# A dense feed-forward block by one level of Strassen's scheme, and a rare branch of the experts with semaphores of its own

## The reference, cut to what matters

```python
def swiglu(t, w_gu, w_down):                 # w_gu: 1024 x 5632, w_down: 2816 x 1024
    a, g = jnp.split(t @ w_gu, 2, axis=-1)
    return (jax.nn.silu(a) * g) @ w_down

def first_block(...):
    ...
    for l in range(DEPTH):                   # DEPTH = 2
        ... mixer, cross attention ...
        if l % 2 == 0:
            f = swiglu(h, ffn_w_gu[l // 2], ffn_w_down[l // 2])
        else:
            f = moe_swiglu(h, moe_router[l // 2], moe_w_gu[l // 2], moe_w_down[l // 2])
        h = layer_norm(ALPHA * h + f, ln_g[l, 2], ln_b[l, 2])

def moe_swiglu(h, w_router, w_gu, w_down):   # 8 experts, 2 for each token
    ...
    for e in range(N_EXPERTS):
        out = out + gate[:, e:e + 1] * swiglu(t, w_gu[e], w_down[e])
```

## Time and profile before

| | us |
|---|---|
| median of three runs | 2226.9 (2225.84 to 2227.3) |
| profiled execution, its own time | 2227.21 |
| profiled execution, span from first to last instruction | 2225.4 |
| TensorE busy in the span | 2157.3 |
| VectorE busy | 511.8 |
| ScalarE busy | 269.4 |
| GpSimd busy | 65.0 |

### The profile page before, as it was taken

One profiled execution on the slowest core, in us unless ns is written; L12 is line 12 of the kernel. 1 busy time (PEld: TensorE's weight loads), 2 busy tenths in 40 slices (PEclk: granted clock), 3 DMA queues, 4 the chain that ended last, 5 costly groups with the idle time before them and its releaser, 6 DMA issues.

```text
span 2225.4 us, 27297 instructions
## 1 busy us (share of the span) xinstructions
PE 2157.3 (97%) x12390; PEld 1211.5 (54%) x12390; DVE 511.8 (23%) x1050; ACT 269.4 (12%) x561; POOL 65.0 (3%) x70
## 2 busy tenths in 40 slices
PE   7999999999999999989999999999999799999998
PEld 3887665987458876753333333333333444854883
DVE  2413213001132232132001001101000489332021
ACT  1242001001013310010000000000000032420000
POOL 0000000000000000000000000000000035000000
PEclk9999999999999999999999999999999899999999
DMA  7524442433245244244999998799999542325240
GB/s 281 217 76 156 185 151 90 176 142 110 107 193 198 95 170 170 76 170 188 384 399 386 393 404 342 306 386 399 383 405 388 208 189 95 114 113 213 90 151 19
DMA packets 38422, 485.39 MB, mean 218 GB/s; under 512 B 4336, under 2 KB 4368, under 8 KB 6816
## 3 DMA queue, kind: packets, MB, share of 16 engines
q1 hardware_dynamic: 34976, 465.70, 52.6%
q0 software_dynamic: 3328, 17.90, 2.0%
HBM read 482.53 MB, written 1.05 MB: 217 GB/s over the span
## 4 chain that ended last, share of the span: by engine, by line
PE 95%; DVE 2%; DMA 1%; ACT 1%; issue 0%; DVEq 0%; SPq 0%; PEldq 0%
PE pair L335 50%; PE bank L335 46%; DMA weights<-in_w_in 0%; DMA weights<-in_even_in 0%; DVE att L1424 0%; DMA norm_par<-in_norms 0%; ACT hT L2255 0%; DVE hT L1424 0%; DVE att L2031 0%; ACT big L2239 0%; DVE stats L1476 0%; DVE h L1485 0%; DVE big L1424 0%; DVE h L1483 0%; DVE big L2013 0%
## 5 line engine op out<-in xcount | busy, mean ns | idle before, releaser
L335 PE MATMUL bank<-weights,att 128*32 128x512 f32 x4224 | 457.8, 593 | 0.0
L335 PE MATMUL pair<-weights,big 128*32 128x512 f32 (+1 forms) x1840 | 340.7, 592 | 1.6 <-DVE big L1911 1.6
L335 PE MATMUL pair<-hT,weights 128*128 128x256 f32 (+1 forms) x1600 | 310.3, 357 | 4.8 <-DVE hT L1424 3.9
L335 PEld LDWEIGHTS bank<-weights,att 128*32 128x32 f32 x4224 | 135.0, 110 | 306.4 <-issue 306.4
L335 PEld LDWEIGHTS pair<-hT,weights 128*128 128x128 f32 x1600 | 276.3, 192 | 38.9 <-DVE hT L1424 4.4
L335 PEld LDWEIGHTS pair<-weights,big 128*32 128x32 f32 (+1 forms) x1840 | 127.6, 129 | 204.5 <-issue 201.9
L335 PE MATMUL bank<-hT,weights 128*128 128x256 f32 x960 | 213.8, 382 | 0.0
L335 PEld LDWEIGHTS bank<-hT,weights 128*128 128x128 f32 x960 | 180.3, 190 | 31.5 <-issue 8.0
L335 PE MATMUL pair<-weights,hT 128*128 128x512 f32 (+1 forms) x448 | 190.6, 586 | 3.3 <-DMA weights<-in_w_in 1.9
L335 PEld LDWEIGHTS pair<-weights,hT 128*128 128x128 f32 x448 | 85.3, 191 | 104.5 <-issue 100.6
L1819 DVE TENSOR_TENSOR big<-head_gain,bank 128x256 f32<-128x256 f32 x66 | 27.8, 421 | 423.9 <-ACT head_gain L2369 423.9
(11 more groups left out here) (277 smaller groups left out, 1384.6 us busy)
## 6 DMA issues: line engine op xcount, KB each, us to landing
weights<-in_moe_up SPq DMA_DIRECT2D x88, 2048.0 KB, 10.7
weights<-in_moe_down SPq DMA_DIRECT2D x40, 2048.0 KB, 11.4
weights<-in_w_in SPq DMA_DIRECT2D x18, 2048.0 KB, 7.4
weights<-in_ffn_up SPq DMA_DIRECT2D x11, 2048.0 KB, 7.3
weights<-in_even_in SPq DMA_DIRECT2D x10, 2048.0 KB, 7.9
weights<-in_mem_wkv SPq DMA_DIRECT2D x8, 2048.0 KB, 7.3
weights<-in_odd_in SPq DMA_DIRECT2D x8, 2048.0 KB, 7.2
norm_par<-in_norms POOLq DMA_DIRECT2D x10, 1024.0 KB, 10.7
```

What stands on the lines that cost most here:

```text
L335: ins = pe.matmul(o, lhsT, rhs, **flags)
```

## The change

The dense block's chunks 2 to 10 are computed by one level of Strassen's scheme, in the form with seven products and fifteen sums. The tokens and the tile of weights are each cut into four blocks; the seven products have 128 moving columns, four tiles of the contraction and two halves of columns, so eight matmuls each. DVE makes four sums of the weights' blocks for each tile, one chunk ahead (`sums_of_tile`), and once four sums of the tokens' blocks (`sums_of_tokens`). The first tile's sums and the tokens' stand ahead of DVE's products for chunks 0 and 1. Some sums of products are left to PSUM, where products 6 and 7 add to the region of product 1 and product 3 to that of product 5; ACT copies the intermediate values out (`kept`), and DVE adds the rest.

In `dense_down` the pair of the second row tile is begun after the first row tile's matmuls of the first tile, and the wait for the last chunk moves to the last tile of weights.

The general path of the experts gets semaphores of its own (`all_filled`, `all_pair0_emptied`, `all0_used`, `all0_landed` and so on). The semaphores of the fast path then count only what it does, in TensorE, DVE and SP; its closing waits and counts on TensorE go, on DVE two of four waits and the counts. The slots' later counts are taken from `few_uses`, 17 for slots 0 and 1 and 34 for the others.

```diff
@@ TensorE: dense_ffn
                 for c in range(2, HID_CHUNKS):
-                    s = next_tile()
-                    o = begin(pairs, (name, "up", c))
-                    for i in range(2):
-                        for part in range(2):
-                            for k in range(KD):
-                                at = k * 512 + part * 256 + i * P
-                                ins = mm(o[:, i, part * T:(part + 1) * T], weights[:, s, at:at + P], hT[:, k, :],
-                                         start=(k == 0), stop=(k == KD - 1))
-                    end(ins)
-                    slot_owed[0] = f"slot{s}_used"
-                pe.wait_ge(*emptied((name, "up", HID_CHUNKS - 1)))
-                dense_down(name)
+                    seven_products(name, c)
+                dense_down(name)
+
+            def seven_products(name, c):
+
+                s = next_tile()
+                o = begin(pairs, (name, "up", c), late=True)
+                w, v = begin(banks, (name, "up", c, 2), late=True), begin(banks, (name, "up", c, 4), late=True)
+                regions = {"Y": o[:, 0, 0:256], "Z": o[:, 1, 0:256], "W": w[:, 0:256], "V": v[:, 0:256]}
+                tile = weights[:, s, :].rearrange("p (k n) -> p k n", n=512)
+                t1, t2, t4 = tile_sums[c % 2]
+
+                def one(label, region, tokens, block, start):
+                    if label not in (2, 4):
+                        jobs[name, "up", c, label] = jobs[name, "up", c]
+                    for i in range(2):
+                        for k in range(KD // 2):
+                            ins = mm(regions[region][:, i * P:(i + 1) * P], block[:, k, i * P:(i + 1) * P], tokens(k),
+                                     start=(start and (i, k) == (0, 0)),
+                                     stop=(k == KD // 2 - 1), skip_group_check=True)
+                    end_late(ins, (name, "up", c, label))
...
+                one(1, "Y", part(0, 0), tile[:, 0:4, 0:256], True)
+                one(2, "W", part(1, 0), tile[:, 4:8, 0:256], True)
+                pe.wait_ge(*L.next("sums_ready"))
+                if c == 2:
+                    pe.wait_ge(*L.next("token_sums_ready"))
+                one(5, "Z", total(0), t1, True)
+                one(4, "V", part(1, 1), t4, True)
+                pe.wait_ge(*L.next("first_kept"))
+                one(6, "Y", total(1), t2, False)
+                pe.wait_ge(*L.next("fifth_kept"))
+                one(3, "Z", total(3), tile[:, 4:8, 256:512], False)
+                pe.wait_ge(*L.next("sixth_kept"))
+                one(7, "Y", total(2), tile[:, 0:4, 256:512], False)
@@ TensorE: dense_down
-                outs = [begin(pairs, (name, "down", t), late=True) for t in range(NT)]
+                outs = []
...
                     for t in range(NT):
+                        if k0 == 0:
+                            outs.append(begin(pairs, (name, "down", t), late=True))
...
+                            if (t, i) == (0, 0) and k1 + nk == KF:
+                                pe.wait_ge(*emptied((name, "up", HID_CHUNKS - 1)))
@@ TensorE: moe, the end of the Else branch
                     few_sum(1)
-                    assert begun() == IN_FEW, begun()
-
-                    for i in range(2):
-                        for t in range(NT):
-                            pe.wait_ge(*emptied(("few_sum", 1, i, t)))
-                    pe.sem_inc(sems("banks_filled"), to_come("banks_filled", IN_FEW["banks_filled"]))
-                    for s in range(2):
-                        more = ALL_ROUNDS - few_count(FEW_ROWS - 2 + s, s)
-                        pe.sem_inc(sems(f"slot{s}_landed"), 16 * more)
-                        pe.sem_inc(sems(f"slot{s}_used"), more)
...
+                for s in range(NSLOT):
+                    after_few[s] = few_uses[s]
@@ VectorE: moe, the end of the Else branch
                     few_sum(1, row)
                     for i in range(2):
-                        for t in range(NT):
-                            ve.wait_ge(*emptied(("few_sum", 1, i, t)))
-                    for name, n in IN_FEW.items():
-                        if name != "banks_filled" and to_come(name, n):
-                            ve.sem_inc(sems(name), to_come(name, n))
+                        ve.wait_ge(*emptied(("few_sum", 1, i, 1)))
@@ VectorE: the dense block
+            def sums_of_tokens():
+
+                a11, a12, a21, a22 = [hT[:, 4 * j:4 * j + 4, t * P:(t + 1) * P] for t in range(NT) for j in range(2)]
+                s1, s2, s3, s4 = [token_sums[:, i, :, :] for i in range(4)]
+                link(ve.tensor_tensor(s1, a21, a22, ALU.add))
+                link(ve.tensor_tensor(s2, s1, a11, ALU.subtract))
+                ve.tensor_tensor(s3, a11, a21, ALU.subtract)
+                ve.tensor_tensor(s4, a12, s2, ALU.subtract).then_inc(sems("token_sums_ready"), 1)
...
+            def sums_of_tile(c):
+
+                n = first_ffn_tile + c
+                ve.wait_ge(*L.at(f"slot{n % NSLOT}_landed", 16 * (n // NSLOT + 1)))
...
+                link(ve.tensor_tensor(t1, b12, b11, ALU.subtract))
+                ve.tensor_tensor(b12, b22, b12, ALU.subtract)
+                link(ve.tensor_tensor(t2, b22, t1, ALU.subtract))
+                ve.tensor_tensor(t4, b21, t2, ALU.subtract).then_inc(sems("sums_ready"), 1)
+                ve.wait_ge(*L.next("sums_ready"))
+
+            def crossed_chunk(name, c):
...
+                ve.wait_ge(*filled((name, "up", c, 2)))
+                ve.wait_ge(*L.next("first_kept"))
+                ve.tensor_tensor(c11, p1, w[:, 0:256], ALU.add).then_inc(w_free, 1)
+                if c + 1 < HID_CHUNKS:
+                    sums_of_tile(c + 1)
+                ve.wait_ge(*L.next("fifth_kept"))
+                ve.wait_ge(*emptied((name, "up", c, 4)))
+                ve.wait_ge(*L.next("sixth_kept"))
+                ve.wait_ge(*filled((name, "up", c, 7)))
+                ve.tensor_tensor(c21, p4, y, ALU.add).then_inc(sems("gate_summed"), 1)
+                L.passed("gate_summed")
+                ve.tensor_tensor(c12, p6, z, ALU.add)
+                link(ve.tensor_tensor(c22, p5, y, ALU.add))
+                for t, up in enumerate((c12, c22)):
+                    ve.wait_ge(*L.next("silu_done"))
+                    ins = ve.tensor_tensor(hidT[:, 2 * c:2 * c + 2, t * P:(t + 1) * P],
+                                           silu[:, c % 2, t, :].rearrange("p (i n) -> p i n", n=P),
+                                           up.rearrange("p (i n) -> p i n", n=P), ALU.mult)
+                ins.then_inc(free, 1)
+
             def dense_ffn(name):
+                ve.wait_ge(*emptied((("hT", "ffn", 0), 1, 1)))
+                sums_of_tile(2)
+                sums_of_tokens()
                 for c in range(HID_CHUNKS):
+                    if c >= 2:
+                        crossed_chunk(name, c)
+                        continue
@@ ScalarE: the dense block
+            def crossed_chunk(name, c):
+
+                o, _ = bank((name, "up", c))
+
+                def keep(i, label, region, done):
+                    act.wait_ge(*filled((name, "up", c, label)))
+                    act.activation(kept[:, i, :], region, ACT.Copy).then_inc(sems(done), 1)
+
+                def gate(t, ready):
+                    act.wait_ge(*ready)
+                    act.activation(silu[:, c % 2, t, :], crossed[:, t, :], ACT.Silu).then_inc(sems("silu_done"), 1)
+                keep(0, 1, o[:, 0, 0:256], "first_kept")
+                gate(0, emptied((name, "up", c, 2)))
+                if c > 2:
+                    act.wait_ge(*emptied((name, "up", c - 1)))
+                keep(1, 5, o[:, 1, 0:256], "fifth_kept")
+                act.wait_ge(*filled((name, "up", c, 4)))
+                v, v_free = bank((name, "up", c, 4))
+                act.activation(kept[:, 2, :], v[:, 0:256], ACT.Copy).then_inc(v_free, 1)
+                keep(3, 6, o[:, 0, 0:256], "sixth_kept")
+                gate(1, L.next("gate_summed"))
@@ SyncE
             def load(src, width):
 
                 i = n[0]
                 n[0] += 1
-                into(i % NSLOT, i // NSLOT, src, width)
+                into(i % NSLOT, i // NSLOT + after_few[i % NSLOT], src, width)
```

More of the change, by code:

```diff
@@ L319, in program @@
         FEW_STEPS = {"picks_ready": N_GROUPS - 1, "gated_ready": N_GROUPS - 1, "few_silu_done": N_GROUPS * HID_CHUNKS * PASSES}
-        def to_come(name, count):
-            return max(EACH[name], IN_FEW[name]) - count
+        few_uses = [few_count(FEW_ROWS - 2 + s, s) if s < 2 else FEW_ROWS for s in range(NSLOT)]
         @block.tensor
@@ L1056, in loop_experts @@
             def loop_experts(n, per, body):
-                before = (filled[0], list(pairs.uses), list(banks.uses), tiles_used[0])
-                pairs.next = banks.next = 0
+                before = (filled["all_filled"], list(all_pairs.uses), list(all_banks.uses), all_tiles[0])
                 with L.loop(n, per):
```

(39 more changed lines are left out.)

176 lines of the change are left out of this document (95 added, 81 removed).

## The result

| | before | changed |
|---|---|---|
| median, us | 2226.4 | 2204.8 |
| lowest to highest, us | 2224.2 to 2227.3 (4 executions) | 2204.1 to 2205.3 (4 executions) |
| span of the profiled execution, us | 2225.4 | 2202.3 |

The change makes the kernel faster: ratio 0.9905 [0.9891, 0.9919], which is 18 to 24 us of 2226.4. The medians differ by 21.6 us, the spans of the two profiled executions by 23.1; 22.6 was forecast, and a time of 2204.3.

What follows compares the result with a forecast made beforehand. TensorE, busy for 97% of the span, was taken to bound the kernel. Gains of 11.8 + 1.6 + 9.2 = 22.6 us gave 2204.3 us, with its own range 2200 to 2209 and an overall range of 2200 to 2214.

Steps and rivals of the forecast that it cites:

- Nine chunks, 11.8 us: Dense block, TensorE's chunks 2 to 10: 112 records at 0.1117 take 12.51 us against 13.82, gaining 11.8 us in nine.
- the start of the down products, 1.6: End of the dense block: TensorE's 1.61 us wait for DVE's product after the last chunk goes, gaining 1.6 us.
- 9.5% and not 12.5%: Dense block chunks: cutting arithmetic from 32/32 to 28/32 is worth 9.5% at the spacing of 128-column records, not 12.5%.
- No wait in the block: Dense block: copies and sums are ready before TensorE wants them, so waits cost nothing; the tightest, `sixth_kept`, has 1.2 us.
- DVE's 6.6 us: Dense block: slack between DVE finishing the next tile's sums, at 9.5 us, and the next chunk's product 5 wanting them, at 16.1.
- the other bound, 5.4 us of restarts: Dense block: upper cost of waits, one 0.2 us restart at each of three fresh waits in nine chunks, 5.4 us.
- The even stage, 9.2 us: End of the experts: the first `even_in` load goes out earlier, so TensorE starts at `normed`, 1757.5, not 1766.69; gain 9.2 us.
- The clock: Even stage: if the granted clock stays up after the shorter idle, 0.8 us more gain; later gaps may shift 1.8 either way.
- `ssm_w`: Even stage: this load, sharing queues with four tiles, might take 15.5 us and land 0.4 us late at the worst.
- Rival 1: Dense block: a hand-over per chunk, at product 6 to 7, takes back 1.3 us, so chunks gain nothing; 2216.1, chance 0.08.
- rival 2: Even stage gains nothing: something else holds its start, or the clock and `ssm_w` take the gain back; 2213.5, chance 0.06.
- rival 3: Dense block: VectorE becomes the bound if the weights' sums run slow, over 3.0 us each; 2235.7, chance 0.04.

Runs made afterwards that it cites:

- the last run: Changed kernel with the ring of banks begun at 2 after the experts and 16 unread matmuls before the first `normed`; 2200.6 us, 0.9883.

## Why the prediction was right, step by step

- **Nine chunks, 11.8 us, and the start of the down products, 1.6.** Together 13.4 forecast, 13.5 read, by the mechanism forecast. The record's distance of 0.1117, the chunk of 12.51 and the vanished wait of 1.61 are all in the trace. The run with half the columns bears on "9.5% and not 12.5%": at half the distance of a 256-column record (0.2159/2) a chunk would be 112 x 0.0037 = 0.42 us shorter, 3.8 us in nine. What keeps that back is not the moving columns; that it is the load of weights is likely, by the rows above, and not shown.
- **No wait in the block.** The slack of 1.2 us for `sixth_kept` is 1.15 in the trace, and laid bare the hand-over costs 0.64. DVE's 6.6 us are bracketed: 4.9 more cost nothing, 9.8 more cost some 45 us. Of the other bound, 5.4 us of restarts, nothing appeared. The sums took 1.22 us (forecast 1.29); the front-loaded ones end at 411.8 and chunk 0's product behind them at 412.4, with 412 and 412.5 forecast and 421 as the limit.
- **The even stage, 9.2 us.** 9.5 came, but not by the forecast's path. The restart lies 8.5 us earlier: the working asked only for `normed` and the load, and overlooked that the first transposes also want bank 0, which DVE empties 0.61 us after `normed`. In the kernel before this wait lay under the load, which landed 8.0 us after DVE's last sum (1758.69, 1766.65); it became visible when the load left. Row tile 0 then takes 11.0 us and not 10.4, since 5.6 us of it and not 4.3 lie at the lower clock, which leaves 7.8. The shorter second stretch at the lower clock gives 1.7 back: 9.5. So two small losses that the forecast had not counted, 0.7 and 0.6 us, were made good by a gain that stands only in its range. That is luck: with a second stretch as long as before, the total would have been some 21.3 us where 22.6 was forecast, still within the range.
- **The clock.** The forecast kept two cases open, 0.8 better if the clock stayed up and 1.8 either way for later gaps. After an idle time of 4.8 us it did not stay up (0.50), and a later gap turned out 1.7 better. With the clock kept up by the last run's matmuls, DVE decides 9.8 us after the first start; 9.6 was forecast, from 1757.48 to 1767.1. The 1.7 is not a property of the changed kernel: the run with four more sums has the same even stage and the same gap of 2.32 us, and there the second stretch is 6.8 us long again (1764.8 to 1771.6). Why it is 3.4 us long in some executions and 6.8 in others is open; no run told it apart. The windows view of the run with four more sums:

```profile
1766.00:1771.00 5.00, 5.00 (x9) 1.97 (x8) 4.62 (x7) 1.97 (x4) 0.00 (x0) 0.50 0.83 315
```

- **`ssm_w`.** It was forecast to be 0.4 us late at the worst, with 15.5 us to land. It took 13.1 and nothing waited for it: L2109's row follows TensorE's transposes in the chain.
- **The rivals.** Rival 1 (the chunks gain nothing) and rival 2 (the even stage gains nothing) fall with the runs of each part alone, 14.2 and 9.4 us. Of rival 3 it is shown that DVE can become the bound, and its condition was unmet: with POOL silent, all sums ran at 1.22 us. No run made POOL work beside them. From 417 to 530 us ACT made 36 copies and 17 operations of Silu in turns and loaded no table. A reload, where this case has one, lasts 1.28 us, and the next activation follows directly (1784.29 and 1785.58 before), so the forecast's 1.3 fits the rows. The Trainium skill, "ScalarE: Activation LUTs", section "Table sets: the hidden batching unit", where copy belongs to every set, agrees with the absence of reloads. By the same page of the Trainium skill, section "What ACT_TABLE_LOAD costs", a switch of sets costs 2.66 us with its drain, which the forecast's 1.3 left out; the rows show no such drain.

## What to carry to other kernels

Fewer multiplications are worth only what is left at the smaller tile's own distance between records: a row of that tile in the kernel before gave the gain of the large edit to 1%. Where a stall is taken away, ask for everything else that the stalled instruction wants, its output bank too, since that lay hidden behind the thing that the profile names. Where a count on a semaphore stands in a queue can be worth much: four moved lines alone gave 7.5 us, and the whole change gave 21.6. And where two traces are compared, count from the last place ahead of the edit: of a difference of 1.4 us in the spans of two executions, 1.2 lay ahead of it.

## What the runs showed of the hardware that was not expected

- A 32-bit matmul of 64 moving columns with a 128x128 load is no faster than one of 128 columns: 1.79 us per 16 records in both. With 8 moving columns 16 records take the same 1.95 us from the start of the first to the end of the last.
- With eight more sums, TensorE idled 2.7 to 2.9 us in each of the chunks 3 to 10, and each time the granted clock then stood at 0.50 for about 3.4 us, beginning some 1 us after TensorE's restart. At that level the records are 0.222 us apart instead of 0.1117 (16 in 3.55 us, from 421.51 to 425.06 in that run). The windows view of that run, after the gap before 460.68 and further on in the same chunk:

```profile
462.00:463.00 1.00, 1.00 (x7) 1.00 (x7) 1.00 (x4) 0.10 (x1) 0.00 (x0) 0.50 0.00 0
...
467.00:470.00 3.00, 3.00 (x29) 3.00 (x28) 2.93 (x3) 0.38 (x1) 0.00 (x0) 1.00 0.00 0
```

- Sixteen matmuls with no use in a gap of 4.3 us kept the granted clock at 1.00 there and at the next gap, and bought 2.5 us from the last `few_sum` to the end (472.8 to 470.3).
- The copy from PSUM by ACT between two groups of matmuls on one region costs TensorE 0.64 us when bare, for 0.38 us of copy.
